# Attention: GpSimd takes a head's low parts after the fourth item instead of after the second

## The chip, the cores and the metric

The kernel runs on one core of a Trainium2 chip. Its engines are TensorE (PE in the rows, PEld its weight loads), VectorE (DVE), ScalarE (ACT), GpSimd (POOL) and SyncE (SP, which issues most transfers). Each has its own instruction stream, in order; they meet by semaphores. The metric is the device time of one execution, in microseconds, where lower is better.

## What is computed

Four transformer layers over 512 tokens of width 1024. Two of them hold a sparse attention, 8 heads of 64, in which each query sees 128 selected keys; one holds a band attention, 16 heads of 64, with a relative bias. The reference of the sparse one, cut:

```python
s = einsum('bqhd,bqkhd->bqhk', qb, k_sel) * hd ** -0.5
s = where(valid, s, -inf)
p = softmax(s, axis=-1)
out = einsum('bqhk,bqkhd->bqhd', p, v_sel)
```

Everything else (input products, retention, mLSTM, RWKV, delta-rule, mixture of experts, MLP) is left as it is.

## The kernel before, in words

All three attentions are one function, `softmax_attention` (L968), called as "sparse_attention" with 8 heads (twice, the first two layers) and as "band_attention" with 16. The work is a list of items (h, t): head h and one of ST = 4 blocks of 128 query rows, so item n is h = n // 4, t = n % 4. Block t sees (t + 1) * 128 keys, so the four items of a head have widths 128, 256, 384 and 512. A stage ends with all engines meeting.

Products are made in single precision from two rounded parts: hi, a rounded copy (ACT), and lo, the raw value less hi. So each head needs hi and lo of its queries, and each pair of heads hi and lo of its keys.

The path of an item n, with the names and the lines:

- PE `scores(n)` (L1011 to L1013): three products q_hi k_hi, q_hi k_lo, q_lo k_hi. For t = 0 it waits for the head's low parts (`ql`, L1006), and for a free bank (mask of n - 3).
- DVE `mask(n)` (L1089): adds the bias and takes the row maximum.
- ACT `exponentials(n)` (L1146): exp and row sums; it waits for the turn of item n - 5, whose buffer it takes.
- DVE `row_sum(n)` (L1094): the reciprocal of the sums. In DVE's order it stands behind mask(n + 1).
- POOL normalising (L1064): rows times the reciprocal.
- PE `turn(n)` (L1021): transposes blocks into PSUM; it waits for the normalising of n. In PE's order it stands behind scores(n + 4).
- ACT `probs_hi(n)` (L1152) and DVE `probs_lo(n)` (L1101): the two parts of the turned probabilities. In ACT's order probs_hi(n) stands before exponentials(n + 4); in DVE's, probs_lo(n) behind mask(n + 4) and row_sum(n + 3).
- PE `head(h)` (L1032): eight products with the values, after the low part of the head's last item, in PE's order behind scores and turn of iteration n = 4h + 9, that is behind turn(4h + 5) and ahead of scores(4h + 10).
- ACT `move(h)` (L1138), DVE `head_sum(h)` (L1106): put the head's output together.

The operands of head h + 2 are prepared this way. ACT `operands_hi(h + 2)` (L1131 the keys, for an even head alone; L1132 the queries) stands behind exponentials(4h + 3). POOL `operands_lo(h + 2)` waits for it (`qh`), subtracts the keys' high part if the head is even (L1054), then the queries' (L1057), and these release scores(4h + 8). The order on POOL is written out in the loop at L1061: normalise item n; for n < 4 also the values' low part (`values_lo`, L1048; the band's are 128x1024, the sparse 128x512); and after one item of each head, `operands_lo` for the head two further on. Heads 0 and 1 are prepared by DVE (L1076). POOL prepares 6 heads in each sparse stage and 14 in the band stage, half of them even. SP carries only the band's bias in these stages.

Of the kernel before, what the change touches and what calls it, by code (L numbers as in the profile page):

```python
# [19 lines left out]
ST = S // P  # L20
# [947 lines left out]
def softmax_attention(K, name, heads, q, k, v_raw, v_parts, scale, bias, out, tiles, k_hi, more_p, bias_source=None):  # L968
# [75 lines left out]
    def g_(g):  # L1044
        def values_lo(t):
            g.wait_ge(vh.sem, vh.at(t + 1))
            raw, hi, lo = v_raw(t), v_parts(None, t)[0], v_parts(None, t)[1]
            g.tensor_tensor(lo, raw, hi.bitcast(F32), ALU.subtract).then_inc(vl.up(), 1)  # L1048

        def operands_lo(h):  # L1050
            if h >= 2:
                g.wait_ge(qh.sem, qh.at(prepared(h)))
                if h % 2 == 0:
                    g.tensor_tensor(k(h // 2)[1], k(h // 2)[0], k_hi(h // 2).bitcast(F32), ALU.subtract).then_inc(ql.up(), 1)  # L1054
                    g.wait_ge(ql.sem, ql.at(prepared(h) - 1))
                g.wait_ge(no.sem, no.n)
                g.tensor_tensor(q_part(h, 1)[rows(h), :], q(h), q_part(h, 0)[rows(h), :].bitcast(F32),  # L1057
                                ALU.subtract).then_inc(ql.up(), 1)
                g.wait_ge(ql.sem, ql.at(prepared(h)))

        for n in range(N):  # L1061
            g.wait_ge(rs.sem, rs.at(n + 1))
            w = (items[n][1] + 1) * P
            g.tensor_tensor(p(n)[:, 0:w], p(n)[:, 0:w], col(n, 3).to_broadcast([P, w]), ALU.mult).then_inc(no.up(), 1)  # L1064
            if n < ST:
                values_lo(n)
            if n % ST == 1 and n // ST + 2 < heads:
                operands_lo(n // ST + 2)

    def v_(v):  # L1070
# [54 lines left out]
    def s_(s):  # L1125
# [29 lines left out]
        for n in range(N + 7):  # L1155
# [10 lines left out]
            if n >= 10 and n % ST == 2:  # L1166
                move(n // ST - 2)

    K.stage(name, sync=sync_, tensor=pe_, vector=v_, scalar=s_, gpsimd=g_)


# [2155 lines left out]
```

## Time and profile before

| | us |
|---|---|
| median of 3 runs | 3919.66 (3915.97 to 3921.26) |
| the profiled execution, its own time | 3916.84 |
| its span | 3915.1 |
| busy PE, DVE, ACT, POOL in the span | 3370.1, 2300.3, 1317.4, 600.3 |
| first sparse attention, about | 351 to 421 |
| second sparse attention, about | 1239 to 1308 |
| band attention, about | 3295 to 3429 |

The busy times say how loaded an engine is over the whole span; the three attention stages, some 270 us together, are read by themselves, in order of time. Busy PE over a stretch can count pipelined products whole, so starts of instructions are compared rather than busy shares.

### The profile page before, as it was taken

Reading aid. Unit: us, or ns where it says so; the run is one execution under the profiler, and the core shown is the slowest. Engines: PE = TensorE matmul, PEld = TensorE weight load, DVE = VectorE, ACT = ScalarE, POOL = GpSimd, SP = SyncE. Lnnn points to the kernel's source line nnn. Section 1 sums busy time; section 2 is a strip of 40 time slices with the busy share of each in tenths; the row PEclk is TensorE's granted clock in tenths of the full one; section 3 lists DMA queues with packets and bytes.
Section 4 is the critical chain, followed back from the end, with each engine's and each line's share of the span. In section 5 each row is a group of like instructions: output and inputs, shape, how many; then the busy total and the mean of one; then the engine's idle time right before and its main releaser. Section 6 shows DMA issues by size and latency. Waiting matters only on the chain. (4 is left out here: it accounts for less than half of the span.)

```text
span 3915.1 us, 43423 instructions
## 1 busy us (share of the span) xinstructions
PE 3370.1 (86%) x16996; PEld 2724.0 (70%) x16996; DVE 2300.3 (59%) x3588; ACT 1317.4 (34%) x1863; POOL 600.3 (15%) x538
## 2 busy tenths in 40 slices
PE   8976788997987778998974886879999998699998
PEld 7863567885863557886844885767778787577787
DVE  7868647995667746994357664454443433653534
ACT  2123525772123524773111112122222324632222
POOL 0025401000015501001013241201100002611000
PEclk8987788999995788999986987789999998999999
DMA  7620004992520004991210000002222221122222
GB/s 272 237 87 0 1 17 185 375 356 83 194 97 0 1 17 161 374 367 47 97 69 1 1 1 1 1 1 92 86 86 97 86 90 54 31 92 77 95 97 75
DMA packets 59580, 401.34 MB, mean 103 GB/s; under 512 B 6769, under 2 KB 8433, under 8 KB 12273
## 3 DMA queue, kind: packets, MB, share of 16 engines
q1 hardware_dynamic: 53616, 356.62, 25.2%
q0 software_dynamic: 5760, 41.95, 3.0%
q8 instruction: 135, 2.21, 0.2%
q14 instruction: 69, 0.56, 0.0%
HBM read 396.45 MB, written 2.10 MB: 102 GB/s over the span
## 5 line engine op out<-in xcount | busy, mean ns | idle before, releaser
L135 PE MATMUL ps<-t_part,weight_hi 128*128 128x512 f32 x2160 | 865.7, 401 | 70.1 <-DVE scr_part L180 38.4
L137 PE MATMUL ps<-t_part,ring_lo 128*128 128x512 f32 x2160 | 853.7, 395 | 0.0
L136 PE MATMUL ps<-scr_part,weight_hi 128*128 128x512 f32 x1648 | 653.1, 396 | 0.0
L347 DVE TENSOR_TENSOR ring_lo<-ring,weight_hi 128x2048 fp32r<-128x2048 f32 x133 | 306.6, 2305 | 387.6 <-ACT weight_hi L340 387.6
L135 PEld LDWEIGHTS ps<-t_part,weight_hi 128*128 128x128 f32 x2160 | 414.5, 192 | 163.8 <-DVE ring_lo L167 70.0
L340 ACT CAST weight_hi<-ring 128x2048 fp32r<-128x2048 f32 x133 | 253.7, 1908 | 694.3 <-PE ps L137 694.3
L137 PEld LDWEIGHTS ps<-t_part,ring_lo 128*128 128x128 f32 x2160 | 413.2, 191 | 88.4
L136 PEld LDWEIGHTS ps<-scr_part,weight_hi 128*128 128x128 f32 x1648 | 318.0, 193 | 69.5 <-issue 3.9
L136 PE MATMUL ps<-big_part,weight_hi 128*128 128x512 f32 x512 | 200.4, 391 | 0.0
L201 POOL TENSOR_TENSOR big<-big 128x512 f32<-128x512 f32 x28 | 48.0, 1713 | 891.2 <-ACT big L194 887.7
L449 DVE SCALAR_TENSOR_TENSOR scr_q<-t,c_act,scr_q 128x256 f32<-128x256 f32 x294 | 142.6, 485 | 10.5
L3015 DVE SCALAR_TENSOR_TENSOR big<-ps,rstd 128x512 f32<-128x512 f32 x64 | 44.2, 690 | 162.3 <-PE ps L137 162.2
L477 POOL DMA_DIRECT2D t<-in_w_ada x40 | 21.5, 539 | 696.5 <-POOLq L85 384.8
L1101 DVE TENSOR_TENSOR scr_rounded<-ps,scr_rounded 128x128 fp32r<-128x128 f32 (+3 forms) x128 | 62.4, 489 | 86.5 <-ACT scr_rounded L1152 84.3
L136 PEld LDWEIGHTS ps<-big_part,weight_hi 128*128 128x128 f32 x512 | 96.8, 189 | 20.1
L1659 ACT COPY scr<-ps 128x512 f32<-128x512 f32 x60 | 35.2, 586 | 220.8 <-PE ps L1626 220.8
L136 PE MATMUL ps<-ring_lo,t_part 128*128 128x256 f32 x384 | 108.7, 283 | 0.0
L137 PE MATMUL ps<-weight_hi,scr_part 128*128 128x256 f32 x384 | 108.7, 283 | 0.0
L135 PE MATMUL ps<-weight_hi,t_part 128*128 128x256 f32 x384 | 108.7, 283 | 0.0
L1064 POOL TENSOR_TENSOR t<-t,cols 128x128 f32<-128x128 f32 (+1 forms) x103 | 71.7, 717 | 217.2 <-DVE cols L1094 215.5
L2081 DVE TENSOR_TENSOR t_part<-t,weight_hi 128x2048 fp32r<-128x2048 f32 x42 | 95.9, 2284 | 0.0
L2081 DVE TENSOR_TENSOR ring_lo<-ring,weight_hi 128x2048 fp32r<-128x2048 f32 x42 | 95.8, 2284 | 0.0
(615 smaller groups left out, 7228.0 us busy)
## 6 DMA issues: line engine op xcount, KB each, us to landing
ring<-in_w_moe SPq DMA_DIRECT2D x84, 1024.0 KB, 5.0
t<-in_w_moe SPq DMA_DIRECT2D x84, 1024.0 KB, 5.0
ring<-in_w SPq DMA_DIRECT2D x64, 1024.0 KB, 4.8
t<-in_w_ada POOLq DMA_DIRECT2D x40, 1024.0 KB, 5.3
ring<-in_w_in SPq DMA_DIRECT2D x32, 1024.0 KB, 5.4
ring<-in_even_in SPq DMA_DIRECT2D x15, 1024.0 KB, 4.8
ring<-in_qkv SPq DMA_DIRECT2D x12, 1024.0 KB, 4.8
ring<-in_w_out SPq DMA_DIRECT2D x8, 1024.0 KB, 4.9
```

The costliest lines, as they stand in the source:

```text
L135: pe.matmul(bank, w_hi, x_hi, start=first, stop=False)
L136: pe.matmul(bank, w_hi, x_lo, start=False, stop=False)
L137: return pe.matmul(bank, w_lo, x_hi, start=False, stop=last)
L201: g.tensor_tensor(self.spare(0), self.spare(0), self.spare(c), ALU.add).then_inc(self.added.up(), 1)
L340: s.copy(K.w_hi[:, n % 2, :], K.ring[:, g % NSLOT, :]).then_inc(w_hi.up(), 1)
L347: v.tensor_tensor(K.ring_lo[:, g % NSLOT, :], K.ring[:, g % NSLOT, :], K.w_hi[:, n % 2, :].bitcast(F32), ALU.subtract).then_inc(w_lo.up(), 1)
L449: ins = v.scalar_tensor_tensor(out=part, in0=w[:, k, :], scalar=K.c_act[:, k:k + 1], in1=part, op0=ALU.mult, op1=ALU.add)
L1064: g.tensor_tensor(p(n)[:, 0:w], p(n)[:, 0:w], col(n, 3).to_broadcast([P, w]), ALU.mult).then_inc(no.up(), 1)
L1101: v.tensor_tensor(pt(h, 1)[:, blocks, t * P:w], turned(n, w).rearrange("p (b q) -> p b q", q=P), pt(h, 0)[:, blocks, t * P:w].bitcast(F32) ...
L1659: s.copy(X(b), bank(n % 2)).then_inc(xc.up(), 1)
L2081: v.tensor_tensor(moe.slot(s)[1], moe.slot(s)[0], moe.hi(s).bitcast(F32), ALU.subtract).then_inc(w_lo.up(), 1)
L3015: v.scalar_tensor_tensor(out=o, in0=ps, scalar=0.0, in1=K.rstd[:, :], op0=ALU.max, op1=ALU.mult).then_inc(st.up(), 1)
```

## The change

One condition in the loop of POOL's program. The low parts of head n // 4 + 2 are taken behind the normalising of the fourth item (n % 4 == 3) of a head instead of the second (n % 4 == 1). Which instructions run, what each waits for, and the order on the other engines stay the same.

```diff
         for n in range(N):
             g.wait_ge(rs.sem, rs.at(n + 1))
             w = (items[n][1] + 1) * P
             g.tensor_tensor(p(n)[:, 0:w], p(n)[:, 0:w], col(n, 3).to_broadcast([P, w]), ALU.mult).then_inc(no.up(), 1)
             if n < ST:
                 values_lo(n)
-            if n % ST == 1 and n // ST + 2 < heads:
+            if n % ST == 3 and n // ST + 2 < heads:
                 operands_lo(n // ST + 2)
```

POOL's order before, for head h: normalise 4h, 4h + 1, low parts of head h + 2, normalise 4h + 2, 4h + 3. After: normalise 4h, 4h + 1, 4h + 2, 4h + 3, low parts of head h + 2.

## Rows read from the trace of the kernel before

**Rows 1.** What ended PE's idle time before the turns of L1021 (us, times).
```profile
  POOL t L1064: 98.9, 70
  POOL h L1064: 21.9, 18
```
**Rows 2.** Timeline of POOL, band stage (start us, us, engine, line, shapes, idle before).
```profile
3341.33 1.29 POOL L1054 TENSOR_TENSOR big_part<-big,h_rounded 128x512 fp32r<-128x512 f32 x1 [2.83 <-ACT h_rounded L1132]
3342.69 1.25 POOL L1057 TENSOR_TENSOR h_rounded<-big,h_rounded 64x512 fp32r<-64x512 f32 x1
3344.03 1.82 POOL L1064 TENSOR_TENSOR h<-h,cols 128x384 f32<-128x384 f32 x2
```
**Rows 3.** Timeline of DVE, the reciprocals of a head's third and fourth item.
```profile
3338.80 0.16 DVE L1094 RECIPROCAL cols<-cols 128x1 f32<-128x1 f32 x1
3341.15 0.16 DVE L1094 RECIPROCAL cols<-cols 128x1 f32<-128x1 f32 x1
```
**Rows 4.** Timeline of ACT, the high parts of turned items in the same stretch.
```profile
3337.21 0.48 ACT L1152 CAST scr_rounded<-ps 128x384 fp32r<-128x384 f32 x1 [1.02 <-PE ps L1021]
3338.92 0.59 ACT L1152 CAST scr_rounded<-ps 128x512 fp32r<-128x512 f32 x1
3341.15 0.26 ACT L1152 CAST scr_rounded<-ps 128x128 fp32r<-128x128 f32 x1
3345.62 0.48 ACT L1152 CAST scr_rounded<-ps 128x384 fp32r<-128x384 f32 x1 [2.91 <-PE ps L1021]
```
**Rows 5.** Timeline of ACT, high parts at the end of the band stage.
```profile
3412.87 0.48 ACT L1152 CAST scr_rounded<-ps 128x384 fp32r<-128x384 f32 x1 [1.01 <-PE ps L1021]
3414.59 0.59 ACT L1152 CAST scr_rounded<-ps 128x512 fp32r<-128x512 f32 x1
3418.39 0.48 ACT L1152 CAST scr_rounded<-ps 128x384 fp32r<-128x384 f32 x1 [0.20 <-PE ps L1021]
```
**Rows 6.** Timeline of DVE there, the low part of the 512-wide item.
```profile
3415.21 0.69 DVE L1101 TENSOR_TENSOR scr_rounded<-ps,scr_rounded 128x512 fp32r<-128x512 f32 x1 [0.58 <-ACT scr_rounded L1152]
```
**Rows 7.** Timeline of PE there: head products, first score product, turn.
```profile
3415.95 1.49 PE L1032 MATMUL ps<-scr_rounded,big_part 128*128 128x512 f32 x8 [0.99 <-DVE scr_rounded L1101]
3417.28 0.39 PE L1011 MATMUL ps<-h_rounded 128*128 128x384 f32 x1
3417.86 0.49 PE L1021 MATMUL ps<-ident,h 128*128 128x128 f32 x3
```
**Rows 8.** Instructions of L1064 (ns min/median/max, first and last start, forms).
```profile
L1064 POOL TENSOR_TENSOR t<-t,cols x103: 398/616/1042, 356.9 to 3420.2; 128x128 f32<-128x128 f32 x26, 128x256 f32<-128x256 f32 x26, 128x384 f32<-128x384 f32 x26, 128x512 f32<-128x512 f32 x25
```
**Rows 9.** Timeline of ACT, high parts of first items: items 8, 24; 8, 24; 8, 56.
```profile
377.34 0.26 ACT L1152 CAST scr_rounded<-ps 128x128 fp32r<-128x128 f32 x1
...
406.72 0.25 ACT L1152 CAST scr_rounded<-ps 128x128 fp32r<-128x128 f32 x1
...
1265.57 0.26 ACT L1152 CAST scr_rounded<-ps 128x128 fp32r<-128x128 f32 x1
...
1294.51 0.26 ACT L1152 CAST scr_rounded<-ps 128x128 fp32r<-128x128 f32 x1
...
3326.30 0.26 ACT L1152 CAST scr_rounded<-ps 128x128 fp32r<-128x128 f32 x1
...
3415.79 0.25 ACT L1152 CAST scr_rounded<-ps 128x128 fp32r<-128x128 f32 x1
```
**Rows 10.** Timeline of PE, head 0 of the band stage and what follows.
```profile
3318.80 2.59 PE L1032 MATMUL ps<-scr_rounded,big_part 128*128 128x512 f32 x8
3321.18 0.46 PE L1011 MATMUL ps<-h_rounded 128*128 128x384 f32 x1
```
**Rows 11.** Timeline of ACT, item 6 of the first sparse stage.
```profile
373.39 0.48 ACT L1152 CAST scr_rounded<-ps 128x384 fp32r<-128x384 f32 x1 [1.32 <-PE ps L1021]
```
**Rows 12.** Windows, end of the band stage (busy us by engine, then PEclk, DMA share, GB/s).
```profile
3415.00:3430.00 15.00, 8.07 (x47) 6.50 (x47) 9.69 (x28) 8.95 (x24) 4.41 (x6) 1.00 0.01 2
```
**Rows 13.** The page's group of POOL additions beside the input products.
```profile
L201 POOL TENSOR_TENSOR big<-big 128x512 f32<-128x512 f32 x28 | 48.0, 1713 | 891.2 <-ACT big L194 887.7
```

## The prediction
> **What bounds the attention now.** I read four views in this order. First, who ends TensorE's idle time before the turns: GpSimd's normalising, for 98.9 + 21.9 = 120.8 us in 88 waits over the three stages [rows 1]. Idle time may cost nothing, so next come the timelines of one stretch of the band stage, engine by engine. VectorE's reciprocal for a head's third item is ready at 3338.80 + 0.16 = 3338.96 [rows 3], but its normalising starts only at 3344.03 [rows 2]: 5.1 us late. In between GpSimd sits idle for 2.83 us waiting for ScalarE's high parts, then spends 3341.33 to 3344.03 = 2.70 us on two subtractions [rows 2]. The reader is to see that a wait at the head of an in-order queue holds back work behind it that was ready all along.
>
> Third, does anybody suffer? ScalarE stands still for 2.91 us until the third item is turned, and one head earlier for 1.02 us [rows 4]. The two kinds alternate: an even head has two subtractions (keys and queries), an odd one has only the queries', so its stall is shorter. No engine is full in that time, so the stall is on the path. Fourth, the last heads of the stage, where nothing is prepared any more, show the pace without it: 3412.87 to 3418.39 = 5.52 us a head [rows 5]. With preparation the band stage takes 3415.79 - 3326.30 = 89.49 us for 12 heads, 7.46 each; the sparse stages take 29.38 and 28.94 us for 4 heads, 7.35 and 7.24 each [rows 9].
>
> **What the 5.52 us is made of.** It is a loop over four engines. From the high part of the 384-wide item to that of the 512-wide one 3412.87 to 3414.59 = 1.72 on ScalarE [rows 5]; to VectorE's low part 0.62 [rows 6]; to the head's products 0.74, their issue 1.33, the next scores 0.58 [rows 7]; the turn and the hand-over to ScalarE 0.53, at 3418.39 [rows 5, 7]. Sum 5.52. So without GpSimd's stall the head's products on TensorE, between two of its waits, are what closes the loop.
>
> **The change, part by part.** Nothing is added or removed: 26 preparations (13 even, 13 odd) move behind two normalisings each. Instructions and semaphores are the same, and no transfer is touched.
>
> *What goes: the stall before items 4h + 2 and 4h + 3.* Both are normalised as soon as their reciprocals exist, and GpSimd's idle wait for ScalarE's high parts is filled with them. What is late next? ScalarE's own work. Call A the start of its 512-wide high part, 3338.92. From there through the operand copies to the point where it would take the next 384-wide item if that were turned it is 3345.62 - 2.91 - 3338.92 = 3.79 us [rows 4], for an even head, the heavier one. The loop above takes 5.52 - 1.72 = 3.80 for the same piece. So ScalarE just keeps pace with the loop and hides its copies; with two chains of equal length I add 0.03 and take 5.55 us for a head.
>
> *What comes: the low parts are ready later.* Even preparation: the fourth item's reciprocal ends at 3341.31, A + 2.39 [rows 3]. I allow 0.1 for the hand-over. Its normalising takes 1.04 [rows 8], to A + 3.5. Keys 1.36 and queries 1.34 (start to start [rows 2]): A + 6.2. Now they lie behind the wait for nothing, since ScalarE's copies end before A + 2.41, where GpSimd started today [rows 2]. Queued behind them on GpSimd are the normalisings of items 4h + 4 and 4h + 5, 0.40 and 0.61 [rows 8]: A + 7.2. And behind those, on TensorE: scores(4h + 8), turn(4h + 4), scores(4h + 9), turn(4h + 5) and then head(h), whose products close the loop. They would be due at A + 5.52 + 0.62 + 0.74 = A + 6.9; with 0.2 for turn(4h + 5) they start at A + 7.4. So an even preparation costs 0.5 us. An odd one has no keys (1.36 less): A + 6.0, hidden with 0.9 to spare. The scores of the first item themselves, released at A + 6.2, have to be masked before the next head's reciprocal, 2.2 after the next A (3341.15 - 3338.92 [rows 3]), at A + 7.7, and cost nothing. If my 0.1 and 0.2 were 0 the cost is 0.2; the far end I take from the rival below.
>
> *The heads between the anchors of [rows 9].* Band, 12 heads, 6 even preparations: 12 x 5.55 + 6 x 0.5 = 69.6 against 89.5: 19.9 saved. Sparse, 4 heads and 2 even preparations: 22.2 + 1.0 = 23.2 against 29.38 and 28.94: 6.2 and 5.7 saved.
>
> *Ahead of the anchors,* the first preparation (head 2) shares GpSimd with the low parts of the values. The instructions up to item 4 are the same in sum, only permuted, so item 4 is normalised at the same time. In the band stage head(0) then follows at the low clock (3318.80 to 3321.18 = 2.38 [rows 10]) and scores(8) now stands late in front of it: I take 0.3 lost; from 0.3 lost to 1.7 gained is possible, if the clock comes back earlier. In the sparse stages, with values half as wide, ScalarE waits 1.32 before item 6 [rows 11]; between 0 and 1.3 of it goes; I take 0.7 for each. *Behind the anchors* nothing was prepared before either: 0.
>
> **Sum.** 19.9 - 0.3 + 6.2 + 0.7 + 5.7 + 0.7 = 32.9 us. Against the profiled execution's own 3916.84 us (span 3915.1) that is 3883.9. The median of the runs lies 2.8 above that execution, so the predicted median is 3919.66 - 32.9 = 3886.8.
>
> **A rule weighed.** GpSimd's 128x512 subtractions last 1.29 us here [rows 2], but the additions of the same size beside the input products last 1.71 on average [rows 13]; in that stage VectorE subtracts two SBUF tensors, in the attention each of its tensor instructions has one operand in PSUM. The Trainium skill, "GPSIMD Engine Reference", the table of what the engine has, says that its SBUF interfaces are shared with VectorE and that there is contention when VectorE's instruction has two SBUF inputs or runs in a two-port mode. By that rule nothing slows here, as VectorE's instructions stay the same, and the trace agrees with 1.29 us. By the row of 1.71, taken as if the rule were wrong, the sum is that of rival 1.
>
> **Rivals.**
> 1. *GpSimd becomes the bound.* It has 4.7 us of uninterrupted work (A + 2.5 to A + 7.2) from the reciprocal to item 4h + 5 with only 0.5 missing already. If packed behind each other its instructions ran 1.71 / 1.29 = 1.33 times as long, or more hand-overs lay between, an even preparation would cost 1.6 more: 10 x 1.6 = 16 less saved, 17 us, 3903. For it: two chains besides are tied within 0.05. Against it: GpSimd is idle today for 2.83 us in just this place [rows 2], and its subtraction takes 1.29 us although VectorE and ScalarE work beside it.
> 2. *The late low parts are hidden altogether.* Then 5 us more, and the two starts give theirs (2.0 and twice 0.6): 41 saved, 3878.5. Against it: scores(4h + 8) stands in front of everything else on TensorE.
> 3. *The change has no effect:* the third item's turn was held by something else as well, as the low part of item n - 3 or the bank. 3920. Against it: ScalarE takes the turned item 5.1 + 1.6 us behind its reciprocal, with GpSimd's end in between.
> 4. *Slower: the clock stays low.* TensorE's two levels cost 1.33 and 2.38 us for the same eight products [rows 7, 10], a factor 1.79. If with its work spread evenly the chip granted 1.2 GHz throughout the stages, the loop's terms on TensorE (1.33 + 0.58 + 0.53 = 2.44) would be 4.37, and a head 7.45 + 0.25 for the late operands = 7.7: 20 x 0.3 = 6 us lost, and the 4 or so undisturbed heads at the ends lose 1.9 each: some 13 us slower, 3933. It decides from about three quarters of the time at the low level. Against it: in the last two heads, with just the pace I forecast, the granted clock was 1.00 [rows 12]. For it only that the stages start at the low level.
>
> **Chances.** My case 0.70, with its own range 3880 to 3893 (a head at 5.5 to 5.75, a preparation at 0.2 to 0.9); rival 1 (3893 to 3910) 0.15; rival 2 (below 3880) 0.08; rival 3 0.05; rival 4 0.02. A measurement of this kernel tells 0.2%, 7.8 us, from no change. Faster by more than that: 0.93; within it 0.05; slower 0.02. The range 3877 to 3899 holds my case, most of rival 2, and the nearer part of rival 1.
>
> **What would show it.** Right: TensorE's waits for GpSimd before turns fall from 120.8 us to a third or less, most of it in the first heads of each stage; ScalarE's high parts of first items lie 5.55 and about 6.05 us apart in turn; the normalising of the third item starts within 0.2 us of its reciprocal; head(h) after an even preparation starts directly behind turn(4h + 5), which is released by GpSimd, and after an odd one it is released by VectorE; the three stages are shorter by 19.6, 6.9 and 6.4 us; the clock is 1.00 there except at the start. Wrong: equal head periods (the lateness is hidden), periods over 6.3 (GpSimd is the bound), a new wait of TensorE before L1011 of a first item that VectorE's mask then waits for, or stages after the attentions that give time back.

## The result, and the profile after

The changed kernel takes 3886.68 us (median of 4 runs, 3883.08 to 3887.98) against 3919.51 before (4 runs); the ratio is 0.9914, 95% interval [0.9902, 0.9927], so some 29 to 38 us less. 3886.8 was predicted. Its profiled execution took 3885.99 us, with a span of 3884.2. In what follows a pair is an even and an odd head together, and the stages are the three attention stages.

What TensorE waited for ahead of its instructions, before the turns (L1021) and before the score products (L1011). The first pair answers to [rows 1]:

```profile
  POOL t L1064: 17.5, 19
  POOL h L1064: 3.6, 4
```

```profile
  POOL h_rounded L1057: 24.3, 14
  POOL big_part L1057: 21.8, 12
```

120.8 us of waiting before turns became 21.1, and 46.1 us of waiting for GpSimd's low parts came in. Before the change that second kind did not exist. The view counts a wait twice, once for the weight load (PEld) and once for the product (PE) behind it, as the same waits in the band stage show (us, times, longest):

```profile
PEld ps L1011 <- POOL h_rounded L1057: 13.1, 7, 4.2
...
PE ps L1011 <- POOL h_rounded L1057: 11.2, 7, 3.7
```

So the 26 entries are 13 waits, one for each even preparation; an odd one is hidden, as forecast. Idle time is not lost time: a product's wait of 1.25 us in an even head of the band stage goes with a head that is only 0.5 us longer.

GpSimd in the band stage, which answers to [rows 2]:

```profile
3327.94 1.04 POOL L1064 TENSOR_TENSOR h<-h,cols 128x512 f32<-128x512 f32 x1 [1.46 <-DVE cols L1094]
3328.94 1.29 POOL L1054 TENSOR_TENSOR big_part<-big,h_rounded 128x512 fp32r<-128x512 f32 x1
3330.32 1.26 POOL L1057 TENSOR_TENSOR h_rounded<-big,h_rounded 64x512 fp32r<-64x512 f32 x1
3331.65 1.76 POOL L1064 TENSOR_TENSOR t<-t,cols 128x128 f32<-128x128 f32 x3
```

The idle 2.83 us for ScalarE are gone from the even preparation. GpSimd now waits 1.46 us for a reciprocal, with nothing held back behind it but, for the last 0.1 us, the subtractions: ScalarE's copies end at 3327.81. The last row is three normalisings, of 128, 256 and 384 columns. TensorE in the same head:

```profile
3331.63 0.33 PE L1011 MATMUL ps<-h_rounded 128*128 128x128 f32 x1 [1.25 <-POOL h_rounded L1057]
...
3332.68 0.44 PE L1021 MATMUL ps<-ident,t 128*128 128x128 f32 x2
...
3332.87 1.48 PE L1032 MATMUL ps<-scr_rounded,big_part 128*128 128x512 f32 x8
...
3334.77 0.49 PE L1021 MATMUL ps<-ident,t 128*128 128x128 f32 x3
```

The head's first scores start when the queries' low part is ready, and the head's products start straight behind turn(4h + 5), with no wait for VectorE. That is the 0.5 us that was predicted for an even preparation. The time from one head to the next is read from ScalarE's high parts of the third items; [rows 5] showed 5.52 us for the undisturbed head, [rows 4] the stalls:

```profile
3323.76 0.48 ACT L1152 CAST scr_rounded<-ps 128x384 fp32r<-128x384 f32 x1 [0.46 <-PE ps L1021]
3329.27 0.48 ACT L1152 CAST scr_rounded<-ps 128x384 fp32r<-128x384 f32 x1
3335.29 0.48 ACT L1152 CAST scr_rounded<-ps 128x384 fp32r<-128x384 f32 x1 [0.47 <-PE ps L1021]
3340.81 0.48 ACT L1152 CAST scr_rounded<-ps 128x384 fp32r<-128x384 f32 x1
```

5.51, 6.02, 5.52: a pair of heads takes 11.53 us where it took twice 7.46 on average. The first items, which answer to [rows 9]:

```profile
377.44 0.25 ACT L1152 CAST scr_rounded<-ps 128x128 fp32r<-128x128 f32 x1
...
399.06 0.25 ACT L1152 CAST scr_rounded<-ps 128x128 fp32r<-128x128 f32 x1
...
1258.38 0.26 ACT L1152 CAST scr_rounded<-ps 128x128 fp32r<-128x128 f32 x1
...
1279.99 0.26 ACT L1152 CAST scr_rounded<-ps 128x128 fp32r<-128x128 f32 x1
...
3316.19 0.26 ACT L1152 CAST scr_rounded<-ps 128x128 fp32r<-128x128 f32 x1
...
3384.32 0.26 ACT L1152 CAST scr_rounded<-ps 128x128 fp32r<-128x128 f32 x1
```

Sparse 21.62 and 21.61 us (23.2 forecast), band 68.13 (69.6 forecast). The windows of the band stage (PE, PEld, DVE, ACT, POOL busy, then PEclk):

```profile
3326.00:3341.00 15.00, 12.42 (x78) 10.61 (x77) 12.62 (x48) 13.93 (x41) 11.41 (x14) 1.00 0.20 52
3341.00:3356.00 15.00, 11.84 (x77) 9.82 (x75) 12.13 (x45) 13.90 (x37) 12.72 (x16) 1.00 0.19 54
```

The granted clock is 1.00, and ScalarE is busy 93% of the time, which suggests that the next bound is close; e10 and e11 test it. Before the change the granted clock fell in some heads (0.89 in the mean of 3341.00:3356.00), and some pairs in which it fell took up to 15.6 us instead of 14.85. Those dips went with the stall. Added up over the third items of the three stages they are 2 to 3 us of what the change saves, an estimate.

### The profile page after: what moved, and what is told of

It reads as the page before. It is cut to its first block and busy times, and to the rows that moved or that the text cites. A ratio compares the mean times of both kernels' runs of the same rounds, so it can differ in the third digit from the quotient of the medians.

```text
span 3884.2 us, 43423 instructions
## 1 busy us (share of the span) xinstructions
PE 3371.6 (87%) x16996; PEld 2720.4 (70%) x16996; DVE 2298.7 (59%) x3588; ACT 1317.1 (34%) x1863; POOL 601.3 (15%) x538
## 5 line engine op out<-in xcount | busy, mean ns | idle before, releaser
L1064 POOL TENSOR_TENSOR t<-t,cols 128x128 f32<-128x128 f32 (+1 forms) x103 | 72.6, 719 | 230.8 <-DVE cols L1094 229.2
L2011 PE MATMUL ps<-weight_hi,big_part 128*128 128x512 f32 x232 | 93.0, 401 | 0.0
```

The costliest lines, as they stand in the source:

```text
L2011: pe.matmul(products(n), h_hi, hi[:, kk, :], start=(k == 0), stop=False)
```

## The experiments

Single runs of this kernel scatter by about 0.2%, and most differences between the changed kernels are no larger. So each kernel is read by its profile as well: by the pair period in the band stage, and by the three attention stages together (each from the start of the last VectorE instruction ahead of it to that of the first one behind; 276.6 us in the first profile of before, 239.1 after). A ratio is to runs of before taken in the same session; e10 and e11 rest on two runs each.

| kernel | median, us | ratio to before, 95% | band pair, us | three stages, us | all else in the span |
|---|---|---|---|---|---|
| before, first profile | 3919.51 | | 14.85 to 15.6 | 276.6 | 3638.5 |
| before, second and third | 3925.59, 3919.67 (one run each) | | | 276.0, 275.3 | 3647.8, 3642.6 |
| after | 3886.68 | 0.9914 [0.9902, 0.9927] | 11.53 | 239.1 | 3645.1 |
| e1 after again | 3889.65 | 0.9915 [0.9901, 0.9929] | 11.52 | 239.3 | 3650.6 |
| e2 sparse only | 3904.90 | 0.9961 [0.9949, 0.9974] | | 260.2 | 3649.5 |
| e3 band only | 3900.35 | 0.9955 [0.9943, 0.9968] | | 255.6 | 3643.0 |
| e4 keys early | 3888.84 | 0.9917 [0.9902, 0.9932] | 11.47 | 237.8 | 3648.2 |
| e6 keys early 2 | 3883.42 | 0.9912 [0.9898, 0.9925] | 11.22 | 237.7 | 3635.6 |
| e7 after third | 3904.28 | 0.9963 [0.9950, 0.9976] | 13.64 | 260.6 | 3641.3 |
| e8 keys twice | 3914.47 | 0.9992 [0.9982, 1.0001] | 13.9 to 14.3, once 12.7 | 264.6 | 3643.6 |
| e9 next first | 3888.35 | 0.9909 [0.9891, 0.9926] | 11.63 | 243.1 | 3646.4 |
| e10 half head | 3883.45 | 0.9898 [0.9877, 0.9919] | 11.07 at full clock | 233.4 | 3645.8 |
| e11 half head, early keys | 3877.96 | 0.9884 [0.9863, 0.9905] | 11.10 | 228.9 | 3648.1 |

**Does it add up, and is anything given back? e1, e2, e3.** e1 is the change once more; e2 and e3 have it in one kind of stage:

```diff
-            if n % ST == 3 and n // ST + 2 < heads:
+            if n % ST == (1 if bias_source else 3) and n // ST + 2 < heads:     # e2; e3 with 3 and 1 exchanged
```

> The change as it is, a second time, for a tighter ratio and a second profile. Theory (the stall in front of the third item is gone, an even preparation costs 0.5 us): the three attention stages are some 38 us shorter than before, the whole 33. What lies between: work outside of the attentions takes 5 to 8 us more, either by chance of one execution (then this profile has another amount) or because of the change (then the same amount again).

> The new order in the two sparse attentions alone; in the band attention the low parts are taken behind the second item, as before. If the savings are local and add up: 15 to 17 us less than before in the stages, ratio about 0.9957. If a later stage gives the time back (the clock, a transfer that lands at its own time): well under 12 us.

> The new order in the band attention alone. Local and additive: 21 us less than before, ratio about 0.9946, and together with the sparse-only kernel the whole 33 to 38 us. If the band stage gains only because its surroundings moved: another amount than 21.

Against the first profile of before, e2's stages are 16.4 us shorter and e3's 21.0; together 37.4, which is the change's own 37.3 to 37.5. By the ratios they save 15.3 and 17.6 us, and e1 33.3 with an interval of 28 to 39. So the savings are local and add up, and in e2 and e3 the stages left as they were keep their length within 0.6 us. e1 had the longer "all else" again (3650.6), which looked as if the change gave time back elsewhere; e5 and e12 were to tell.

**Chance outside the attentions. e5, e12**, the kernel before, unchanged.

> The kernel before, a second profile, to see how much the stages that the change does not touch vary from one execution to the next. In the kernels with the change the work between the second sparse attention and the band attention was 3 to 6 us longer than in the first profile of before. If that is chance of the first profile: longer here too, and the attention stages the same within 0.6 us. If the change causes it: as in the first profile.

> The kernel before once more, a third profile, for the stages outside the attentions: they should again differ by several us from one of the two others while the attention stages agree within about 1 us with the first.

With the same code, all else takes 3638.5, 3647.8 and 3642.6 us, 9 us apart, and in the kernels with the change anything from 3635.6 to 3650.6. The stages of the three profiles of before lie within 1.3 us (1 was expected). So differences of this size outside the attentions come with the execution. The first profile of before was at its short end, so the two spans differ by 30.9 us where the stages differ by 37.5; nothing is given back that these profiles can show.

**What an even preparation costs. e4, e6.** The keys' parts are taken early; only the queries' stay behind the fourth item.

```diff
+            if n % ST == 1 and n // ST % 2 == 0 and n // ST + 2 < heads:
+                keys_lo(n // ST + 2)                       # GpSimd, both kernels
             if n % ST == 3 and n // ST + 2 < heads:
                 operands_lo(n // ST + 2)                   # queries alone
...
+                if n % ST == 1 and n // ST % 2 == 0 and n // ST + 2 < heads:
+                    keys_hi(n // ST + 2)                   # ScalarE, e4
+                    if n // ST % 2 == 1 and n // ST + 3 < heads:
+                        keys_hi(n // ST + 3)               # ScalarE, e6: inside n % ST == 3, head 2 at n == 0
```

> On top of the change: the keys' high part (ScalarE) and low part (GpSimd) of an even head are taken two items earlier, behind the second item, where ScalarE's wait for the scores is long fulfilled; only the queries stay behind the fourth. Theory that an even preparation costs 0.5 us since 1.36 us of the keys' subtraction stand ahead of turn(4h + 5) and the head's products: head periods become equal at 5.5 us, band pair 11.0 instead of 11.5, in all 4 to 5 us less than the change, ratio to before about 0.990. Rival that ScalarE's copies or VectorE are the bound of the even heads: the pair stays at 11.5. Rival that the third item's turn is late again: pair over 11.5.

ScalarE in e4 (the L1161 rows are the third items of three heads in turn, L1133 is the copy of the keys, L1155 the exponentials):

```profile
3327.45 0.48 ACT L1161 CAST scr_rounded<-ps 128x384 fp32r<-128x384 f32 x1 [0.21 <-PE ps L1021]
...
3331.74 0.40 ACT L1155 ACTIVATE h<-t,cols 128x128 f32<-128x128 f32 x1 [0.35 <-DVE cols L1094]
...
3332.90 0.61 ACT L1133 CAST h_rounded<-big 128x512 fp32r<-128x512 f32 x1
3333.41 0.47 ACT L1161 CAST scr_rounded<-ps 128x384 fp32r<-128x384 f32 x1
...
3338.92 0.48 ACT L1161 CAST scr_rounded<-ps 128x384 fp32r<-128x384 f32 x1 [0.20 <-PE ps L1021]
```

5.96 and 5.51: the expected gain did not come. The third item at 3333.41 no longer waits for TensorE; ScalarE is late itself. It waits 0.35 us for VectorE's mask and then makes the copy (L1133), where with the change the copies stand ahead of that wait and fill it. GpSimd's 0.5 us were exchanged for ScalarE's.

> As the first kernel with early keys, but ScalarE rounds an even head's keys one head earlier, behind the queries of the odd head, where it waits 0.35 us for VectorE's mask anyway; GpSimd still subtracts behind the second item. In the first kernel the head with the copy behind its second item took 5.96 us, the other 5.51. Theory that only the copy's place behind the wait for the mask spoiled it: both heads 5.5, the band pair 11.0, 4 to 5 us less than the change in the three stages. Rival that ScalarE is full at 5.5 with both copies in one head and any place costs 0.4: pair 11.4 to 11.5, nothing gained.

```profile
3342.99 0.48 ACT L1161 CAST scr_rounded<-ps 128x384 fp32r<-128x384 f32 x1 [0.20 <-PE ps L1021]
...
3348.66 0.46 ACT L1161 CAST scr_rounded<-ps 128x384 fp32r<-128x384 f32 x1
...
3354.21 0.48 ACT L1161 CAST scr_rounded<-ps 128x384 fp32r<-128x384 f32 x1 [0.20 <-PE ps L1021]
```

5.67 and 5.55: the pair fell by 0.3 instead of the expected 0.5, and the stages are 1.5 us shorter than with the change, not 4 to 5. The head with both copies is paced by ScalarE, which idles 0.1 us in it. The ratio's interval covers that of the change: as a version it is not shown to be faster.

**The order on GpSimd, one item either way. e7, e9.**

```diff
-            if n % ST == 3 and n // ST + 2 < heads:
+            if n % ST == 2 and n // ST + 2 < heads:                  # e7
+            if n % ST == 0 and n >= ST and n // ST + 1 < heads:      # e9, operands_lo(n // ST + 1)
```

> The low parts behind the third item (n % 4 == 2), between before and the change. Theory: the third item is free, the fourth's normalising waits for the low parts; in even heads it ends at A + 6.2 and its turn comes 1.3 us late, in odd heads it is hidden: band pair 12.4 against 14.85 before and 11.5 with the change; 8 to 9 us slower than the change, 28 to 30 faster than before in the stages. Rival that what matters is only whether GpSimd idles for ScalarE with ready items behind it: same pair as before. Rival that earlier operands pay: faster than the change.

TensorE in an even head of e7, and a window of it:

```profile
3336.30 0.66 PE L1021 MATMUL ps<-ident,h 128*128 128x128 f32 x4 [1.77 <-POOL h L1064]
...
3338.36 2.61 PE L1032 MATMUL ps<-scr_rounded,big_part 128*128 128x512 f32 x8 [0.17 <-DVE scr_rounded L1101]
...
3340.77 0.51 PE L1011 MATMUL ps<-h_rounded 128*128 128x384 f32 x1
```

```profile
3339.00:3340.00 1.00, 1.00 (x4) 0.91 (x3) 0.90 (x7) 0.64 (x4) 0.99 (x1) 0.50 0.00 0
```

The order of the three is as predicted (13.64 between 11.53 and 14.85), but the pair is 1.2 longer than the 12.4 worked out. ScalarE's wait for the fourth item's turn was 1.44 us, as good as the 1.3 expected. The rest is the clock: behind the wait it fell to 0.50, 1.2 GHz, in every even head of the band stage behind the first, and the eight head products took 3340.77 - 3338.36 = 2.41 us to issue instead of 1.32 (3334.19 less 3332.87 in the profile after). One even head of the first sparse stage kept the clock at 1.00 behind a wait of 1.76 us; it took 6.92 us (third items at 392.45 and 399.37) where those of the second sparse stage, in which it fell, took 7.96 and 8.04.

> The low parts one item later still: behind the normalising of the next head's first item (4h + 4), for head h + 2. Theory by the same arithmetic: even preparation, normalising of the fourth item to A + 3.5, of the next to 3.9, keys and queries to 6.6, the second item's to 7.2; TensorE has scores(4h + 8) only from A + 6.6 and comes to the head's products about 0.3 later than with the change: band pair 11.7 to 12.0 against 11.5; with the clock staying at 1.00, 2 to 4 us slower than the change. Rival that only the normalising of the second item counts: the same pair, 11.5. Rival that the long wait before the scores lowers the clock: pair 12.7 or more.

The pair is 11.63, just under the range, the stages 3.9 us longer than with the change. TensorE waits 1.59 us for the low parts and the clock stays at 1.00. So the low parts, one item later, cost 0.1 us a pair, by way of the first item's scores that stand ahead of the head's products.

**Double the suspected cost. e8.** One more subtraction of 64x512 in each even preparation:

```diff
                 if h % 2 == 0:
+                    g.tensor_tensor(q_part(h, 1)[rows(h), :], q(h), q_part(h, 0)[rows(h), :].bitcast(F32), ALU.subtract)
                     g.tensor_tensor(k(h // 2)[1], k(h // 2)[0], k_hi(h // 2).bitcast(F32), ALU.subtract).then_inc(ql.up(), 1)
```

> On top of the change every even preparation has one more subtraction of 64x512 on GpSimd (1.36 us, results the same). Theory that even preparations end directly ahead of the head's products: each costs its whole 1.36, the band pair is 12.9 instead of 11.5, in all 14 to 18 us slower than the change. Rival that the 0.5 us come from elsewhere and GpSimd has slack: pair under 12.2. Rival that GpSimd then is the bound in odd heads too: over 13.5.

```profile
3341.16 0.33 PE L1011 MATMUL ps<-h_rounded 128*128 128x128 f32 x1 [2.45 <-POOL h_rounded L1058]
...
3342.74 2.59 PE L1032 MATMUL ps<-scr_rounded,big_part 128*128 128x512 f32 x8
...
3345.12 0.45 PE L1011 MATMUL ps<-h_rounded 128*128 128x384 f32 x1
```

```profile
3343.00:3344.00 1.00, 1.00 (x4) 0.81 (x4) 0.63 (x4) 0.87 (x3) 0.94 (x1) 0.50 0.00 0
```

The stages are 25 us longer than with the change and five of six pairs take 13.9 to 14.3, where 14 to 18 us and 12.9 were expected: 1.36 us of GpSimd work cost 2.4 to 2.8 a pair. TensorE's wait grew by 1.2 (1.25 to 2.45), the direct cost; the clock then fell, and the head products took 2.38 us, another 1.05. The sixth pair separates the two prices. Its wait is the same 2.45 us, but the clock stays at 1.00:

```profile
3383.34 0.33 PE L1011 MATMUL ps<-h_rounded 128*128 128x128 f32 x1 [2.45 <-POOL h_rounded L1058]
...
3384.58 1.47 PE L1032 MATMUL ps<-scr_rounded,big_part 128*128 128x512 f32 x8
...
3385.89 0.39 PE L1011 MATMUL ps<-h_rounded 128*128 128x384 f32 x1
```

```profile
3384.00:3385.00 1.00, 1.00 (x8) 0.86 (x8) 0.89 (x5) 0.79 (x4) 1.00 (x2) 1.00 0.00 0
```

```profile
3379.79 0.48 ACT L1153 CAST scr_rounded<-ps 128x384 fp32r<-128x384 f32 x1
...
3387.00 0.48 ACT L1153 CAST scr_rounded<-ps 128x384 fp32r<-128x384 f32 x1 [1.25 <-PE ps L1021]
...
3392.51 0.48 ACT L1153 CAST scr_rounded<-ps 128x384 fp32r<-128x384 f32 x1
```

7.21 and 5.51 make 12.72, 1.2 more than with the change and close to the 12.9 expected. So the direction, the place and the direct price were right, and the low clock doubled the price where it came. By the stages the extra work eats two thirds of the gain, by the medians nearly all of it (0.9992; the profiled execution, 3910.02 us, was below its kernel's median).

**Who closes the loop? e10, e11.** The products with the low part of the probabilities are left out, in the change and in e6:

```diff
-                for lo in range(2):
+                for lo in range(1):
                     ins = pe.matmul(K.ps[:, 4 + h % 2, b * P:S], v_parts(h, b), pt(h, lo)[:, b, b * P:S],
```

> On top of the change the head's products are four instead of eight: those with the probabilities' low part are left out (the low part is still made). Each head's products are 0.67 us shorter. Theory of two nearly equal chains: the stretch from TensorE's late start to the next turn gets 0.67 shorter, but ScalarE's and VectorE's chain of 5.5 a head takes over; pair 10.9 to 11.1 instead of 11.5. Rival that TensorE's products alone close the loop: 1.33 less a pair, 10.2.

> The four head products instead of eight, with the second kernel of early keys, whose pair was 11.2. If ScalarE's and VectorE's own work is what is left of the 11.2: the pair stays within 10.9 to 11.2. If TensorE still closed the loop there: 10.2 or less.

ScalarE's third items, first in e10, then in e11:

```profile
3344.51 0.46 ACT L1152 CAST scr_rounded<-ps 128x384 fp32r<-128x384 f32 x1
...
3349.99 0.46 ACT L1152 CAST scr_rounded<-ps 128x384 fp32r<-128x384 f32 x1
...
3355.58 0.46 ACT L1152 CAST scr_rounded<-ps 128x384 fp32r<-128x384 f32 x1
```

```profile
3331.91 0.47 ACT L1161 CAST scr_rounded<-ps 128x384 fp32r<-128x384 f32 x1
...
3337.75 0.46 ACT L1161 CAST scr_rounded<-ps 128x384 fp32r<-128x384 f32 x1
...
3343.01 0.46 ACT L1161 CAST scr_rounded<-ps 128x384 fp32r<-128x384 f32 x1
```

Where the clock is 1.00 the pair is 11.07 and 11.10, though TensorE has 1.3 us less in it: both inside their ranges, and the rival's 10.2 is out. In e10 that holds for two of six pairs of the band stage (10.9 and 11.1); in the other four the clock fell, and they took 11.8 to 12.3. In e11 it stayed at 1.00. ScalarE waits for nobody in front of these rows, and in all it idles about 0.6 us in such a pair. So at the full clock the pair could not have come much under 11.1, and the loop over TensorE's products is only one of two chains of nearly equal length.

## Why the prediction was right, point by point

- *The stall and its removal.* Right. The waits before turns fell to a sixth, and the stages together save 37.5 us by the first profiles. The 120.8 us that the forecast began with were read too large: they count weight loads and products both, and the products alone waited 52.5 us.

```profile
  PEld ps L1021: 68.3, 56
  PE ps L1021: 52.5, 32
```

- *The third item within 0.2 us of its reciprocal.* So in every other head only (0.14 us). In the head behind an even preparation GpSimd is still working off its queue, and the third normalising starts 1.55 us late:

```profile
3330.87 0.16 DVE L1094 RECIPROCAL cols<-cols 128x1 f32<-128x1 f32 x1
```

The reciprocal ends at 3331.03; the last of GpSimd's three normalisings from 3331.65 on ends at 3333.41. It costs nothing, since TensorE takes that turn at 3334.77, behind the head's products. The forecast left this out.

- *5.55 us for an undisturbed head, two chains tied.* Right, with 0.03 too much: 5.51 and 5.52 in the rows after; e10 and e11 show the other chain at 11.1 a pair.
- *An even preparation costs 0.5 us, through turn(4h + 5) and the head's products.* Right in the band stage: 11.53 for the pair against 2 x 5.52 = 11.04. A, the start of the 512-wide high part on ScalarE, was 3325.5; the products start at 3332.87, A + 7.4 as worked out. In the sparse stages the pair is 388.76 - 377.44 = 11.32 by the first items, so 0.3. e6 shows that taking the keys away gains only 0.3, since ScalarE is next.
- *The heads between the anchors.* Mis-sized: 19.9, 6.2 and 5.7 us were forecast, 21.4, 7.8 and 7.3 came. The first anchor of each stage stands behind ScalarE's copies of keys and queries, the last stands behind none, as nothing is left to prepare; 4 or 12 whole periods therefore count one pair of copies too many, 3327.71 - 3326.68 = 1.03 us on ScalarE in the profile after, in each stage, 3.1 in all. Of the remaining 1.6 half is the cheaper even preparation of the sparse stages (4 x 0.2) and most of the rest the 0.03 a head (20 x 0.03).
- *The starts.* Sparse 0.7 and 0.8 for 0.7 each; band 0.0 for a loss of 0.3. The first items of the stages stand at 361.95, 1250.20 and 3308.34 before, 362.76, 1243.79 and 3298.21 after.
- *Behind the anchors.* 0 was forecast, and the anchors with the starts make 37.9 us, the stages 37.5. The ends of the stages gave 0.5, -0.9 and 0.0 us. From the last anchor to the last item's high part the profiles of before and after all have 8.65 to 8.68 us; what varies is the exit behind it, and between two profiles of before that varies as much (14.3 us from the last anchor of the first stage to the next VectorE work, 13.2 in e5).
- *The sum.* So some 5 us too little were forecast for the stages, and the median fell by 32.8 and not by 37.5. The e5 and e12 profiles put before's stages at 276.0 on average, the saving at 36.8, and all else varies by 15 us from one execution to another: that the median came within 0.2 us of the forecast is in part luck. The interval, 29 to 38, holds both numbers.
- *The rivals.* GpSimd as the bound did not show: its subtractions still take 1.29 us. The low clock did not come with the change, 1.00 in its windows. But its mechanism is real and nearer than I had it: a place one item earlier (e7) brings it in each even head of the band stage, one more subtraction (e8) in five of six.
- *What would show it.* The forecast said a new wait before L1011 would speak against it if the mask then waited. The wait came. In an even head behind the first preparation the mask then waits 0.2 us, so it does not speak against it. The mask's waits for L1013 over all three stages did rise, from 8.7 to 16.2 us (4.0 to 4.5 in the band stage, where 3.4 more stand under another cause); nearly all that is new lies in the first preparation of each stage, where the mask waits up to 3.4 us, and is inside the starts above. The high parts of first items were to lie 5.55 and about 6.05 us apart; they lie 5.24 and 6.28 apart (3316.19, 3321.43, 3327.71), because ScalarE's two copies stand in front of every other one. It is the third items that show 5.5 and 6.0. The stages were to be shorter by 19.6, 6.9 and 6.4 us (band, first, second sparse); they are by 21.4, 8.9 and 7.2.

## What to carry to other kernels

On an in-order engine, put an instruction that waits for another engine behind all work that will be ready earlier, and count what then stands behind it up to the instruction that closes the loop; here GpSimd's lateness reached the loop through eight products far down another engine's queue. When a stall is removed, price the next chain before trying to remove the rest: here it was 0.4 us away, and e4 exchanged one bound for another. And between two marks in a pipeline, count the work on both sides of each mark, not only the periods.

## What the runs showed of the hardware

A wait of TensorE can cost more than its length. With waits of 1.25 and 1.59 us in each even head of the band stage behind the first (after, e9) the granted clock stayed at 1.00, 2.4 GHz. With 1.77 us (e7) it went to 0.50, 1.2 GHz, in each of them, with 2.45 us (e8) in five of six, and the eight products behind took 2.4 us instead of 1.3. The length of the wait alone does not decide it: the 2.45 us of e8 at 3383.34 left the clock at 1.00, and in the kernel before the waits of 2.55 us did so ahead of 3330.06 and not ahead of 3344.91. What does decide it is open here. The Trainium skill, "TensorE: Matmul & The Clock Gate", has in its Part 1 that the throttled state is the default and activity releases it; the traces agree as far as they go, with 0.50 behind longer waits and 1.00 where TensorE was kept busier. GpSimd's subtractions of 64x512 and 128x512 took 1.26 to 1.29 us on average in every kernel, whether VectorE was busy 9.4 or 12.6 of 15 us beside it.
